# First layer of a four-mixer kernel: the gate projection spread over the layer's attention, keys projected last, one output bank

## The reference, cut to what matters

```python
u = rmsnorm(x, norm_pre[0])                                  # 512 x 1024
q, kc, vc, ks, vs, kw, vw, gate, z = jnp.split(u @ w_in, points, axis=-1)
k_cmp = compress(kc, pe_k, w1_k, w2_k)                       # 31 compressed keys per group
v_cmp = compress(vc, pe_v, w1_v, w2_v)
...
# per block of queries: o_c over compressed keys, o_s and o_w over single keys, causal
o = gate[..., 0:1] * o_c + gate[..., 1:2] * o_s + gate[..., 2:3] * o_w
o = o.reshape(b, s, NSA_WIDTH) * jax.nn.silu(z)
return o @ w_out
```

## Time and profile before

| | |
|---|---|
| median of 3 runs | 1393.45 us (1392.7 to 1395.8) |
| the profiled execution: its own time | 1394.15 us |
| the profiled execution: span of the trace | 1392.2 us, clock 0.997 |
| TensorE busy over the span | 96% |
| DVE, ACT, POOL busy over the span | 47%, 53%, 55% |

### The profile page before, as it was taken

The page is one execution under the profiler, slowest core; times in us unless marked ns, Lnnn a source line. Parts: engine busy times, 40 slices in busy tenths (PEclk is TensorE's granted clock), DMA queues, the critical chain, the costliest instruction groups (busy, mean ns, idle before and its releaser), DMA issues.

```text
span 1392.2 us, 20871 instructions
## 1 busy us (share of the span) xinstructions
PE 1338.4 (96%) x7738; PEld 1096.1 (79%) x7738; DVE 653.7 (47%) x1609; ACT 732.5 (53%) x1552; POOL 765.3 (55%) x771
## 2 busy tenths in 40 slices
PE   6999999999999999999999999999999999999997
PEld 5888777777888787878788888778889887778885
DVE  4222068888251454553420012881463347887135
ACT  4244258888343556665433233892544356887252
POOL 4455256667554465665652544686646433686652
PEclk9999999999999999999999999999999999999999
DMA  6232311100434222221443222425226222002322
GB/s 240 102 118 95 121 61 32 32 32 2 167 113 145 90 76 99 79 96 44 168 152 139 104 91 91 152 92 197 80 93 225 91 91 61 2 16 105 137 91 61
DMA packets 28324, 138.65 MB, mean 100 GB/s; under 512 B 3520, under 2 KB 4032, under 8 KB 16960
## 3 DMA queue, kind: packets, MB, share of 16 engines
q1 hardware_dynamic: 14624, 98.05, 20.0%
q10 hardware_dynamic: 13600, 39.27, 8.2%
HBM read 127.86 MB, written 8.39 MB: 98 GB/s over the span
## 4 chain that ended last, share of the span: by engine, by line
PE 75%; DVE 8%; POOL 6%; ACT 6%; issue 2%; DMA 2%; ACTq 0%; SPq 0%; POOLq 0%; DVEq 0%
PE psum L471 51%; PE psum L505 9%; DVE w_free L1460 2%; POOL w_free L1579 2%; ACT w_free L915 2%; PE psum L1407 2%; PE psum L1029 2%; PE psum L1388 2%; PE psum L1360 2%; PE psum L1003 2%; ACT u_hi L1518 1%; DVE u_lo L1473 1%; PE psum L725 1%; POOL split L1596 1%; PE psum L1373 1%
## 5 line engine op out<-in xcount | busy, mean ns | idle before, releaser
L426 POOL TENSOR_TENSOR w_lo<-w_raw,w_hi 128x2048 fp32r<-128x2048 f32 (+2 forms) x154 | 415.6, 2714 | 317.6 <-ACT w_hi L417 308.3
L417 ACT ACTIVATE w_hi<-w_raw 128x2048 fp32r<-128x2048 f32 (+1 forms) x90 | 167.1, 1856 | 94.7 <-DMA w_raw<-in_weights 79.5
L471 PE MATMUL psum<-w_hi,split 128*128 128x512 f32 x608 | 195.2, 394 | 3.0 <-POOL w_lo L426 2.2
L471 PE MATMUL psum<-u_lo,w_hi 128*128 128x512 f32 (+1 forms) x492 | 194.1, 395 | 0.0
L471 PE MATMUL psum<-u_hi,w_hi 128*128 128x512 f32 (+1 forms) x492 | 191.7, 390 | 0.0
L471 PE MATMUL psum<-u_hi,w_lo 128*128 128x512 f32 (+1 forms) x492 | 191.7, 390 | 0.0
L915 ACT ACTIVATE w_free<-w_free,neg_max 128x512 f32<-128x512 f32 (+3 forms) x256 | 148.4, 585 | 10.1 <-DVE neg_max L1460 9.1
L1473 DVE TENSOR_TENSOR u_lo<-psum,u_hi 128x512 fp32r<-128x512 f32 (+3 forms) x256 | 123.8, 519 | 28.9 <-ACT u_hi L1518 26.2
L471 PE MATMUL psum<-w_hi,u_lo 128*128 128x512 f32 (+2 forms) x352 | 134.6, 382 | 1.8 <-DVE u_lo L875 1.8
L471 PEld LDWEIGHTS psum<-w_hi,split 128*128 128x128 f32 x608 | 114.2, 188 | 27.5 <-POOL w_lo L426 3.1
L471 PE MATMUL psum<-w_lo,u_hi 128*128 128x512 f32 (+2 forms) x352 | 132.9, 378 | 0.0
(11 more groups left out here) (216 smaller groups left out, 2503.6 us busy)
## 6 DMA issues: line engine op xcount, KB each, us to landing
w_raw<-in_weights SPq DMA_DIRECT2D x87, 1024.0 KB, 4.8
x<-x_scratch ACTq DMA_DIRECT2D x12, 512.0 KB, 5.2
gain<-in_gains ACTq DMA_DIRECT2D x9, 512.0 KB, 4.7
gain<-in_strips ACTq DMA_DIRECT2D x16, 256.0 KB, 2.9
spare<-in_strips ACTq DMA_DIRECT2D x16, 256.0 KB, 3.0
x_scratch<-x ACTq DMA_DIRECT2D x8, 512.0 KB, 4.1
gain<-in_near ACTq DMA_DIRECT2D x8, 512.0 KB, 4.3
w_raw<-in_near ACTq DMA_DIRECT2D x8, 512.0 KB, 3.7
```

The source lines that it names most:

```text
L417: high = nc.scalar.activation(w_hi[b][:, c], w_raw[b][:, c], ACT.Copy)
L426: low = nc.gpsimd.tensor_tensor(w_lo[b][:, c], w_raw[b][:, c], w_hi[b][:, c].bitcast(F32), ALU.subtract)
L471: mm = nc.tensor.matmul(dst, lhs, rhs, start=(a == 0 and k == 0 and (wl, ul) == (0, 1)), stop=(a + 1 == u and k + 1 == nk and (wl, ul) == ...
```

## The change

The gate projection `nsa_z` is no longer done ahead of the attention. It becomes eight tiles of eight chunks (one tile for each u). Six chunks are done at the start of the attention, and two after the last transposes of each two steps, until all 64 are done (i = 56). One bank, 7, holds the tile; ACT takes it with silu (`z_take`) at step 8t + 3, and the next tile's first chunk waits for that. The weights of z use one ring slot, a tile (128 x 1024) at a time: SP loads, ACT makes the high part (`z_high_part`) and POOL the low part in two pieces (`z_low_part`). Since bank 7 is taken, all groups of the attention put their output into bank 6, and the first product of a group waits until the group before it has been added up.

In front of the attention the order is now values, compressed-side keys (`nsa_kc`), `nsa_q0`, both compression units, the gates, `nsa_q1` with the compressed scores, and the keys of both branches (`nsa_k`) last. The gates' unit is split over 384 columns only. The 16 transposes of the compressed probabilities stand at the start of the attention. The maps' high and low parts lie in the room of x and in a ring slot in place of u's room, and the weights of `nsa_out`: its first unit is split in four parts at steps 60 to 63, its second goes to u's room and is split at the end of the attention.

```diff
-_run("nsa_k", 2, (4, 4), 512, "features")
+_run("nsa_kc", 1, (4, 4), 512, "features")
+_run("nsa_q0", 1, (4, 4), 512, "features")
 _run("nsa_cmp0", 1, (16,), 128, "compress")
-_run("nsa_q0", 1, (4, 4), 512, "features")
 _run("nsa_cmp1", 1, (16,), 128, "compress")
+_run("nsa_gate", 1, (8,), GATES, "features")
 _run("nsa_q1", 1, (4, 4), 512, "features")
-_run("nsa_gate", 1, (8,), GATES, "features")
-_run("nsa_z", 2, (4, 4), 512, "features")
+_run("nsa_k", 1, (4, 4), 512, "features")
+_tiles("nsa_z", [("z", u) for u in range(KC)])
...
+            in_nsa = {Z_UNIT: n - 3, NSA_OUT: n - 1, NSA_OUT + 2: Z_UNIT - 2, NSA_OUT + 3: Z_UNIT - 1, NSA_OUT + 4: NSA_OUT}
+            in_nsa.update((m, m - 1) for m in range(Z_UNIT + 1, NSA_OUT))
...
+            def z_half(t):
+                cols = slice(t % 2 * D, t % 2 * D + D)
+                sp.dma_start(w_raw[SLOT[Z_UNIT]][:, cols], A["weights"][Z_UNIT + t // 2][:, cols]).then_inc(z_loaded[t % 2], 16)
...
+                        if t < 2:
+                            sp.wait_ge(used, count)
+                        else:
+                            sp.wait_ge(z_done, t - 1)
+                        z_half(t)
...
+            if n == RUNS["nsa_gate"]["unit"]:
+                c = slice(0, KC * GATES)
...
+        def out_bank(f, g):
+            return 6 if f is nsa_flow else 6 + g % 2
...
+        Z_FIRST = 6
+        Z_BANK = 7
+
+        def z_step(t):
+
+            return max(0, KC * (t + 1) - Z_FIRST - 1) // 2 * 2 + 1
+
+        def z_home(u):
+            c = (None, N_OUT + 2 * T, N_OUT + 3 * T)[u % 3]
+            return x[:, 7 * T:8 * T] if c is None else at(c, T)
+
+        def z_fill(pe, first, count):
+
+            b = SLOT[Z_UNIT]
+            for c in range(first, min(first + count, KC * KC)):
+                t, k = divmod(c, KC)
+                if k == 0:
+                    pe.wait_ge(z_ready, t + 1)
+                    if t == 0:
+                        pe.wait_ge(cmp_shifted, 1)
+                    else:
+                        pe.wait_ge(z_taken, t)
+                col = t % 2 * D + k * P
+                for nth, (w, u) in enumerate(((w_hi, u_lo), (w_lo, u_hi), (w_hi, u_hi))):
+                    mm = nc.tensor.matmul(bank(Z_BANK), w[b][:, col:col + P], u[:, k * T:(k + 1) * T],
+                                          start=(k == 0 and nth == 0), stop=(k == KC - 1 and nth == 2))
+                if k == KC - 1:
+                    mm.then_inc(z_done, 1)
+
+        def z_high_part(act, t):
+
+            b, c = SLOT[Z_UNIT], slice(t % 2 * D, t % 2 * D + D)
+            act.wait_ge(z_loaded[t % 2], 16 * (t // 2 + 1))
+            nc.scalar.activation(w_hi[b][:, c], w_raw[b][:, c], ACT.Copy).then_inc(z_high, 1)
+            if t == KC - 1:
+                act.sem_inc(w_high, NSA_OUT - Z_UNIT)
+
+        def z_low_part(pool, t, half):
+
+            b, c = SLOT[Z_UNIT], t % 2 * D + half * T
+            if half == 0:
+                pool.wait_ge(z_high, t + 1)
+            low = nc.gpsimd.tensor_tensor(w_lo[b][:, c:c + T], w_raw[b][:, c:c + T], w_hi[b][:, c:c + T].bitcast(F32), ALU.subtract)
+            if half == 1:
+                low.then_inc(z_ready, 1)
+                if t == KC - 1:
+                    pool.sem_inc(w_ready, NSA_OUT - Z_UNIT)
+
+        def z_take(act, t):
+
+            act.wait_ge(z_done, t + 1)
+            if t >= 3:
+                act.wait_ge(nsa_flow.gated, 2 * (t - 2))
+            nc.scalar.activation(z_home(t), bank(Z_BANK), ACT.Silu).then_inc(z_taken, 1)
...
-                if m == 0 and br == 0 and g >= 2:
-                    pe.wait_ge(f.out_sum, 2 * g - 2)
+                held = 1 if f is nsa_flow else 2
+                if m == 0 and br == 0 and g >= held:
+                    pe.wait_ge(f.out_sum, 2 * (g - held) + 2)
...
+            if f is nsa_flow:
+                z_fill(pe, 0, Z_FIRST)
+                for g in range(3):
+                    compress_turn_tensor(pe, g)
...
+                    z_fill(pe, Z_FIRST + i, 2)
+                    if i == 0:
+                        compress_turn_tensor(pe, 3)
...
+                    if i == 2:
+                        compress_turned_high(act, 3)
+                    for t in range(KC):
+                        if i == z_step(t) + 2:
+                            z_take(act, t)
+                        if t >= 2 and i == z_step(t - 2) + 3:
+                            z_high_part(act, t)
+                    if f.steps - 4 <= i < f.steps:
+                        split_high(act, NSA_OUT, i - f.steps + 4, 4)
                 if 0 <= i - 1 < f.steps:
...
+                if f is nsa_flow:
+                    for t in range(2, KC):
+                        if i - z_step(t - 2) - 5 in (0, 1):
+                            z_low_part(pool, t, i - z_step(t - 2) - 5)
+                    if f.steps - 3 <= i <= f.steps:
+                        split_low(pool, NSA_OUT, i - f.steps + 3)
+                    if i == f.steps + LAG + 2:
+                        split_low(pool, NSA_OUT + 1)
...
+            project_tensor(pe, "nsa_kc")
+            project_tensor(pe, "nsa_q0")
+            compress_hidden_tensor(pe, 0)
+            compress_hidden_tensor(pe, 1)
+            project_tensor(pe, "nsa_gate", banks=1, base=6)
+            beside_q1 = {(0, 1, j): beside_last_q(pe, j) for j in range(NT)}
+            beside_q1.update({(0, 0, 1): lambda: gates_tensor(pe), (0, 0, 2): lambda: compress_heads_tensor(pe)})
+            project_tensor(pe, "nsa_q1", between=beside_q1)
+            for j in range(NT):
+                compress_scores_tensor(pe, 1, j)
             project_tensor(pe, "nsa_k")
-            compress_hidden_tensor(pe, 0)
-            project_tensor(pe, "nsa_q0")
-            compress_hidden_tensor(pe, 1)
-            project_tensor(pe, "nsa_q1", between={(0, 0, 2): lambda: compress_heads_tensor(pe)})
-            project_tensor(pe, "nsa_gate", banks=1, base=4)
-            project_tensor(pe, "nsa_z", only=(0,), between={(0, a, j): beside_first_z(pe, a, j) for a in range(2) for j in range(NT)})
-            project_tensor(pe, "nsa_z", only=(1,), between={(1, 1, 2): lambda: compress_turn_tensor(pe)})
```

More of the change, by code:

```diff
@@ L144, in _program @@
         SLOTS = 3
+        U_SLOT = SLOTS
+        Z_UNIT, NSA_OUT = RUNS["nsa_z"]["unit"], RUNS["nsa_out"]["unit"]
         SLOT, BEFORE, NTH = list(range(SLOTS)), [None] * SLOTS, [0] * SLOTS
@@ L213, in _program @@
         LAG = 3
+        PT_SET = 14 * P
         MLA_SCALE = (64 + ROPE) ** -0.5
@@ L415, in split_high @@
             act.wait_ge(w_loaded[b], 16 * (NTH[n] + 1))
-            c = piece(part, parts)
+            c = slice(0, KC * GATES) if n == RUNS["nsa_gate"]["unit"] else piece(part, parts)
             high = nc.scalar.activation(w_hi[b][:, c], w_raw[b][:, c], ACT.Copy)
@@ L2482, in _ @@
             first_pool(pool)
-            for name in ("nsa_v", "nsa_k", "nsa_cmp0", "nsa_q0", "nsa_cmp1", "nsa_q1", "nsa_gate", "nsa_z"):
+            for name in ("nsa_v", "nsa_kc", "nsa_q0", "nsa_cmp0", "nsa_cmp1", "nsa_gate", "nsa_q1"):
                 project_pool(pool, name)
+            for t in range(2):
+                z_low_part(pool, t, 0)
+                z_low_part(pool, t, 1)
             pair_pool(pool, nsa_flow)
```

207 lines of the change are left out of this document (118 added, 89 removed).

## The result

The changed kernel takes 1403.9 us, the median of 4 executions (1401.66 to 1405.38), against 1394.62 for before: a ratio of 1.0066 with an interval of 1.0044 to 1.0087. The forecast was 1383.5. The profiled execution took 1405.38 us, 11.2 more than that of before, where the sum had -10.0. So 21.2 us are to be found.

A forecast was written before the change was run, and what follows sets the result against it. In the attention no engine is full and the four wait in turn, leaving TensorE about 3.05 us of slack a u. The terms -39.7 + 26.8 + 2.1 - 0.7 + 1.5 = -10.0 us give 1383.5 us, range 1375 to 1394.

The forecast's parts named there:

- named signs of being wrong: A u over 23.5, TensorE waiting for silu each tile, front waits of 5 us or more, or clock falling in the attention.
- Taken out of the full stretch: 39.7 us.: In front of the attention: 174 `nsa_z` matmuls at 0.228 us leave for the attention's steps, saving 39.7 us there.
- the stall at `nsa_q1`: In front: TensorE waits 2.1 us for `nsa_q1`'s first unit, ready after 11.4 us with 9.3 us of other work meanwhile.
- the same work stays: In front of the attention: TensorE has no wait there now and its remaining work is unchanged; only a 2.1 us stall comes.
- If TensorE is full, a u is 15.55 + 24 x 0.229 = 21.05: Attention: lower bound of a u with chunks, 21.05 us; with stalls 22.3 was taken, so the attention grows by 26.8 us.
- I take -0.7: Attention's start: chunks fill part of the 9.2 us stretch with idle time and low clock; -0.7 us, bounds 0 and -3.
- Full TensorE: Rival, attention: chunks make the waits for POOL vanish and hide ACT's loads; u 21.05 to 21.8, 1376 us; chance 0.17.
- ACT holds TensorE: Rival, attention: silu and its loads, 3.2 us, lie on the cycle; u 24.2, 1397.5 us, slower; chance 0.13.
- Nothing much: Rival, attention: the single bank adds 0.5 us to each group; u 23.3, -2.7 us, 1391 us; chance 0.15.
- ScalarE's table loads.: ACT in the attention: a switch costs 1.29 us by the trace, not the skill page's 2.66; the trace's figure was used.
- The single output bank ... I cost it at nothing.: Attention: two chunks hide each group's wait for the bank; 0 us, without them up to 1 us in each of 15 groups.
- Together +1.5: Attention's end: first output product waits some 0.7 us, second `nsa_out` unit's POOL split is covered; +1.5 us, 0 to 4.

The follow-up runs named there:

- its own edit: Changed kernel with the second half's compressed scores in four groups of 24 inside the first unit of `nsa_k`, not one run: 1400.31 us, 1.0036.
- the tail's edit: Changed kernel with each quarter of `nsa_out`'s first-unit low part waiting for its own quarter of the high part, not all four: 1398.09 us, 1.0020.
- the copy: Changed kernel with ACT's Copy in place of silu on the gate tiles, so no table loads in the attention; output lacks silu: 1396.35 us, 1.0007.
- the row for 1 matmul: Kernel with both edits, only the last `nsa_z` matmul of each tile left (1 in a u, not 24), z wrong: 1380.32 us, one execution.
- both edits: Changed kernel with `nsa_out`'s low part waiting quarter by quarter and the compressed scores spread inside `nsa_k`: 1394.59 us, 0.9991.
- the single bank alone: Kernel before with only the output of all groups in bank 6 and the wait for the group before, no chunks between: 1395.1 us, 1.0003.

## Why the prediction was wrong, point by point

1403.9 us lies above the range (1375 to 1394) and above the slowest rival (1397.5), whose cause did not come about. The u of 22.77 lies within the forecast's own 21.8 to 23.1; what failed are the tail, the price of the chunks in the attention with its first six steps, and the order in front. Of the named signs of being wrong one came, the clock that falls in the attention, in its first six steps and at its end. With the flaws mended the three stretches of the table make -37.3 + 33.2 + 3.4 = -0.7 us (the front from the trace of its own edit, the other two from that of both): the attention alone takes back nearly all that the front gives.

**"Taken out of the full stretch: 39.7 us."** Right in itself, and so was the stall at `nsa_q1` (2.1 forecast, 1.82 in the trace). The step that failed is "the same work stays" in front: the work stayed, but the 96 small matmuls came to stand in one run, and the lower clock cost 4.5 us by the rows. Undoing that alone brought the first scores 3.0 us forward, and gave 4.2 by the ratios.

**"If TensorE is full, a u is 15.55 + 24 x 0.229 = 21.05."** This term was mis-sized. A chunk inside `nsa_z` costs 0.688, but a pair of chunks between other matmuls costs 1.56, so the four pairs of a u cost 6.25. TensorE's work is 15.55 + 6.25 = 21.8, and 22.77 - 0.93 of stalls gives 21.84. The stalls themselves are smaller than the 1.0 to 1.5 forecast. The u of 22.3 became 22.77, which over 29/4 u is 3.4 of the 7.1 us; the rest, 3.7, lies mostly in the first six steps. There the three pairs of chunks should have cost 3 x 0.92 less the 0.7, so 2.1 us, and 14.40 - 9.20 = 5.2 were spent: the step "I take -0.7" hoped for a gain from filling idle time, and the stretch kept its idle time and its low clock beside the new work. Three pairs at 1.56 are 4.7 of the 5.2, and the four moved transposes 0.5. Two other traces bound the rest: with the tail's edit the clock happens not to fall there, and the stretch takes 13.76 us; with the copy, so without the loads, it takes 13.49. Neither comes near the 9.20 + 2.1 = 11.3 of the forecast.

The rival *Full TensorE* (a u of 21.3) did not come about, and could not: its 21.05 was the same mis-sized term, TensorE's own work is 21.8, and even without any load a u is 22.28. *ACT holds TensorE* did not happen either: the next tile's first chunk waits 0.28 us for the silu, not 3.2. But the row for 1 matmul shows that ACT stood right behind TensorE. *Nothing much* named the single bank, which added nothing.

**"ScalarE's table loads."** A load costs 1.28 to 1.30 with nothing before it (242.12 to 243.42, 244.03 to 245.33), as the earlier trace rows had it. The Trainium skill, page "ScalarE: Activation LUTs", section "What ACT_TABLE_LOAD costs", gives 2.66 for a switch, a load of about 1.28 and a drain of 1.38; the trace agrees on the load and shows no drain behind it. To keep activations of one set together, which the same page of the Trainium skill advises in its section "Table sets: the hidden batching unit", did pay: tanh in place of silu was worth 6.1 us by the ratios, of which the attention's rows show 4.1.

**"The single output bank ... I cost it at nothing."** Right, and the reason given ("what hides it are the two chunks") holds for the changed kernel: with two chunks moved ahead the wait shows. The price without them ("up to 1 us in each of 15 groups") was too high: in the kernel before, without any chunk, 7 waits of at most 0.3 us cost nothing.

**"Together +1.5" for the end.** This is the largest failed step: 8.8 us. I costed the low part of `nsa_out` by its pieces (1.36 each on POOL) and put the last one late by 0.7. I did not ask what the first piece waits for, and who is queued behind it on POOL. `split_low` is not new, and the diff shows only the calls by quarters; the line to read was the `wait_ge(w_high, n + 1)` in it, which all four quarters share. That wait and the low clock behind it are 5.4 of the 7.3 us that the step was off. The other 1.9 stay with both edits; in them the first output product waits 1.54 us for POOL, not the 0.7 of the forecast.

**The unchanged code, +3.5.** In the changed kernel's trace the clock falls again later (0.98 over 400 to 500 us). So it does in ten of the fourteen traces, that of the single bank alone among them, and not with both edits or before; and the kernel before itself ran from 1391.72 us at a mean clock of 0.997 to 1398.53 at 0.992 in 27 executions. So such falls come and go from one execution to the next; how much of the 3.5 the change causes is open.

## What to carry to other kernels

Work moved beside a tuned loop costs what it costs there: measure a block of it from the start of its first instruction to the start of what follows, and sum each engine's new work before counting slack (here a u was 2.3 us longer with hardly a matmul added, and ACT, with its new work, busy in nearly all of it). When a split is done in pieces, follow each piece's wait to the line that raises the semaphore, and then list what is queued behind it on that engine. And when instructions move, look at what now stands in one run: small matmuls that were spread among large ones can take the clock with them.

## What the runs showed of the hardware that was not expected

The clock fell while TensorE was never idle: over 96 matmuls 64x32 in one run (0.69, then 0.50; the two other kernels that keep the run have the fall too), and not over the same matmuls in groups of 24 among products of 128x512 (1.00). At the end of the attention it fell behind an idle time of 2.64 us and within the next of 1.44, and also with the tail's edit alone (behind 0.40 and 1.64 us, 0.50 from 346.0 to 352.8); with both edits (0.41, 1.65 and 1.54) it did not fall. What decides was not found.

Matmuls of 128x512 that follow one another start 0.229 us apart, but the first interval behind a transpose is 0.31 and the last before scores of 64 rows 0.32 us, 0.18 us more for a block of six.
